# Cached keys turned on VectorE, one head at a time, instead of on TensorE: one inference step of a two-layer hybrid decoder

## The reference

```python
def moba_attend(q, kb, vb, t, slopes):
    qf = q * (B_HEAD_DIM ** -0.5)
    kbar = jnp.mean(kb.astype(jnp.float32), axis=2)
    g = jnp.einsum('hqd,hnd->hqn', qf.astype(jnp.float32), kbar)
    ...
    _, top = lax.top_k(g, min(MOBA_TOPK, NB))
    ...
    s = jnp.einsum('hqd,hqnkd->hqnk', qf, ks).astype(jnp.float32) - slopes[:, None, None, None] * dist
    s = jnp.where(valid[..., None] & (dist >= 0), s, NEG)
    p = jax.nn.softmax(s.reshape(H, q.shape[1], -1), axis=-1).reshape(s.shape)
    return jnp.einsum('hqnk,hqnkd->hqd', p.astype(vs.dtype), vs)
```

## Time and profile before

| | |
|---|---|
| median of the three runs | 1226.19 us |
| the profiled execution's own time | 1224.0 us |
| its span, first to last instruction | 1222.3 us |
| mean granted TensorE clock | 0.992 |
| TensorE busy | 1176.9 us, 96% |
| VectorE busy | 713.0 us, 58% |
| ScalarE busy | 564.2 us, 46% |
| DMA | 324.87 MB, mean 266 GB/s |
| key stage | 334.5 to 487.0 us |
| value stage | 487.0 to 634 us |

### The profile page before, as it was taken

One profiled execution on the slowest core, in us unless ns is written; L12 is line 12 of the kernel. 1 busy time (PEld: TensorE's weight loads), 2 busy tenths in 40 slices (PEclk: granted clock), 3 DMA queues, 4 the chain that ended last, 5 costly groups with the idle time before them and its releaser, 6 DMA issues.

```text
span 1222.3 us, 23737 instructions
## 1 busy us (share of the span) xinstructions
PE 1176.9 (96%) x9352; PEld 1042.2 (85%) x9352; DVE 713.0 (58%) x1355; ACT 564.2 (46%) x714; POOL 331.5 (27%) x207
## 2 busy tenths in 40 slices
PE   5899999999999999999999999899999989999997
PEld 2589798878888787787788898899999889999997
DVE  3746555545544546633545447489999996583112
ACT  3333324333354444422333237576666656575443
POOL 1000000000000002200000002667666778605773
PEclk9999999999999999999999999999999999999998
DMA  9999899999898878899999997585848445454542
GB/s 332 339 331 343 283 334 314 375 354 355 290 313 305 277 259 295 258 371 328 338 372 342 321 331 200 174 280 165 283 156 275 138 142 184 140 174 156 166 145 94
DMA packets 236962, 324.87 MB, mean 266 GB/s; under 512 B 12429, under 2 KB 152525, under 8 KB 236429
## 3 DMA queue, kind: packets, MB, share of 16 engines
q1 hardware_dynamic: 233472, 312.78, 75.7%
q0 software_dynamic: 2192, 7.79, 2.2%
q10 hardware_dynamic: 1188, 2.79, 0.7%
HBM read 317.96 MB, written 7.06 MB: 266 GB/s over the span
## 4 chain that ended last, share of the span: by engine, by line
PE 76%; DVE 16%; DMA 3%; issue 2%; ACT 2%; SPq 1%; POOL 0%; DVEq 0%; ACTq 0%
PE PS L307 19%; PE PS L311 18%; PE PS L310 18%; DVE PS L1763 10%; PE PS L395 5%; PE PS L987 4%; DMA XR<-in_ada_w 3%; PE PS L1014 3%; PE PS L1245 2%; DVE WLO L301 1%; PE PS L410 1%; SPq L382 1%; PE PS L1971 1%; ACT WHI L296 1%; DVE PS L1757 0%
## 5 line engine op out<-in xcount | busy, mean ns | idle before, releaser
L307 PE MATMUL PS<-HH,WHI 128*128 128x288 f32 x2176 | 662.4, 304 | 16.7 <-DVE HL L1683 4.5
L311 PE MATMUL PS<-HH,WLO 128*128 128x288 f32 x2176 | 643.9, 296 | 0.0
L310 PE MATMUL PS<-HL,WHI 128*128 128x288 f32 x2176 | 643.7, 296 | 0.0
L307 PEld LDWEIGHTS PS<-HH,WHI 128*128 128x128 f32 x2176 | 410.9, 189 | 38.2 <-issue 32.0
L296 ACT ACTIVATE WHI<-WRAW 128x1024 fp32r<-128x1024 f32 x272 | 283.8, 1056 | 344.1 <-PE PS L311 291.2
L310 PEld LDWEIGHTS PS<-HL,WHI 128*128 128x128 f32 x2176 | 411.2, 189 | 0.0
L311 PEld LDWEIGHTS PS<-HH,WLO 128*128 128x128 f32 x2176 | 410.6, 189 | 0.0
L301 POOL TENSOR_TENSOR WLO<-WRAW,WHI 128x1024 fp32r<-128x1024 f32 x117 | 281.1, 2422 | 192.6 <-ACT WHI L296 192.6
L301 DVE TENSOR_TENSOR WLO<-WRAW,WHI 128x1024 fp32r<-128x1024 f32 x155 | 191.1, 1235 | 158.1 <-ACT WHI L296 157.9
L1763 DVE SCALAR_TENSOR_TENSOR PS<-ACTS,CWT,PS 128x288 f32<-128x288 f32 x448 | 192.5, 516 | 0.0
L1739 ACT ACTIVATE ACTS<-ACTS 128x1088 f32<-128x1088 f32 x32 | 70.4, 2200 | 59.8 <-DVE ACTS L1761 34.6
(11 more groups left out here) (280 smaller groups left out, 748.1 us busy)
## 6 DMA issues: line engine op xcount, KB each, us to landing
XR<-in_ada_w SPq DMA_DIRECT2D x192, 512.0 KB, 8.5
WRAW<-in_ab_w_in SPq DMA_DIRECT2D x112, 512.0 KB, 7.3
WRAW<-in_c_w_in SPq DMA_DIRECT2D x96, 512.0 KB, 3.6
XR<-in_cache_b_k SPq DMA_DIRECT2D x128, 256.0 KB, 5.2
XR<-in_cache_b_v SPq DMA_DIRECT2D x128, 256.0 KB, 5.5
WRAW<-in_ab_w_out SPq DMA_DIRECT2D x32, 512.0 KB, 8.9
WRAW<-in_c_w_out SPq DMA_DIRECT2D x32, 512.0 KB, 3.3
ACTS<-in_x_prompt ACTq DMA_DIRECT2D x2, 1024.0 KB, 11.1
```

The lines of the kernel that those rows point to most:

```text
L307: first = pe.matmul(out, whi, HH[:, k, :], start=start, stop=False)
L310: pe.matmul(out, whi, HL[:, k, :], start=False, stop=False)
L311: return pe.matmul(out, wlo, HH[:, k, :], start=False, stop=stop)
```

## The change

Keys are turned by VectorE: `dve.transpose` turns 32x32 blocks, each within its group of 32 partitions, from `XR` to `KT`, two instructions of 128x512 for a head (all four samples, 256 positions each). `KT` is a ring of five slots, one head each. A key of head dimension 128 then no longer lies with its dimension down the 128 partitions: partition 32 i + d holds, for each position group i of 32, dimension 32 e + d of part e. So the query is spread block-diagonally into `BD` (`q_spread` on TensorE, `q_fill` on VectorE and ScalarE), and a head's scores are 16 matmuls of 64 columns (four samples, four parts e of the dimension). A row of the scores (sample, parity of the head, position group, token) now holds a quarter of a block, 64 positions, for each of the four head pairs side by side; four rows make one softmax. Gate, maximum and sum over the four rows are made by small TensorE operations (`gate_sum`, `max_turn`, `max_back`, `z_sum`), and the probabilities are scaled by ScalarE (`row_norm`) before they are turned. The turning is 36 steps (`probs_turn`), two at a time behind a part (`probs_pair`).

Two heads are scored behind every fourth part. Both slots of a half are released together, when its fourth head has been turned. For b = 0 the probabilities are turned in block 7 and in the first value chunk, for b = 1 in value chunks 8 to 10, and branch A's steps move behind them, its statistic to blocks 3 to 7. The page numbers are read behind the last pages of the block before, in the value stage too. `SBUF` room for the ring (3072 columns) comes from a smaller scratch area for software DMA.

```diff
         HL = sb("HL", [P, KC, R], F32R)
-        NACT = 56 * R
+        NACT = 56 * R + 3072
...
-        KT = A(6912, 4096).rearrange("p (b j h n) -> p b j h n", b=2, j=4, h=2)
...
+        BD = A(5632, 3072).rearrange("p (x w) -> p x w", w=48)
+        OQ = A(5632, 768).rearrange("p (j g w) -> p j g w", j=4, g=4)
+        KT = [A(at, 1024).rearrange("p (x n) -> p x n", x=8) for at in (8704, 9728, 56 * R, 56 * R + 1024, 56 * R + 2048)]
...
+        SROW = [A(at, 4 * 288).rearrange("p (h c) -> p h c", h=4) for at in (3456, 13824)]
...
-        def k_turn(pe, u, c, g4):
...
-            for h2 in range(2):
-                for t in range(2):
-                    at = 512 * (2 * j2 + t) + P * ((2 * hh + h2) % 4)
-                    last = pe.transpose(PS[:, (M2, M3)[g % 2], (2 * h2 + t) * P:(2 * h2 + t + 1) * P],
-                                        XR[:, c, at:at + P], IDENT[:])
-            last.then_inc(kt_tr, 1)
...
+        def k_turn(dve, u, h):
+
+            n, half = 8 * u + h, h // 4
+            if h % 4 == 0:
+                dve.wait_ge(x_rdy[2 * half], need(17 + u, 2 * half))
+                dve.wait_ge(x_rdy[2 * half + 1], need(17 + u, 2 * half + 1))
+            if n >= len(KT):
+                dve.wait_ge(ks_head, n - len(KT) + 1)
+            for c in range(2):
+                dve.transpose(KT[n % len(KT)][:, 4 * c:4 * c + 4, :],
+                              XR[:, 2 * half + c].rearrange("p (a n) -> p a n", a=4)[:, :, P * (h % 4):P * (h % 4) + P]
+                              ).then_inc(kt_tr, 1)
+            if h % 4 == 3:
+                dve.wait_ge(kt_tr, 2 * n + 2)
+                dve.sem_inc(x_used[2 * half], 1)
+                dve.sem_inc(x_used[2 * half + 1], 1)
+
+        def q_spread(pe, b, e):
+
...
+            rhs = Q[:, :, SR0 + 16 * b:SR0 + 16 * b + 16].rearrange("p h (s i) -> p s h i", i=DS)
+            for i in range(4):
+                dst = PS[32 * i:32 * i + 32, M3, P * e:P * e + P].rearrange("p (s h i) -> p s h i", s=4, h=HEADS)
+                last = pe.matmul(dst, IDENT[:, 32 * e:32 * e + 32], rhs, start=True, stop=True)
+            last.then_inc(s_qr, 1)
+
+        def q_fill(eng, b, tokens, pairs=range(4)):
+
+            eng.wait_ge(s_qr, 4 * b + 4)
+            if b:
+                eng.wait_ge(ks_head, 28 if pairs[0] == 0 else 32)
...
+                eng.wait_ge(s_bdz, 1)
+            g0, g1 = pairs[0], pairs[-1] + 1
+            for i in tokens:
+                src = PS[32 * i:32 * i + 32, M3, :].rearrange("p (x g h q) -> p x g h q", g=4, h=2, q=DS)
+                for h2 in range(2):
+                    at = 32 * h2 + DS * i
+                    dst = BD[32 * i:32 * i + 32, :, at:at + DS].rearrange("p (x g) q -> p x g q", g=4)[:, :, g0:g1]
+                    if tokens[0]:
+                        eng.activation(dst, src[:, :, g0:g1, h2, :], ACT.Copy).then_inc(s_bda, 1)
+                    else:
+                        eng.tensor_copy(dst, src[:, :, g0:g1, h2, :]).then_inc(s_bdf, 1)
...
+        def k_scores(pe, u, h):
+
+            g, h2, bank = h // 2, h % 2, (M0, M2)[u % 2]
+            n = 8 * u + h
+            pe.wait_ge(kt_tr, 2 * n + 2)
+            if h == 0:
+                if u > 1:
+                    pe.wait_ge(ks_free, u - 1)
+                if u % 4 == 0:
+                    pe.wait_ge(s_bdf, 4 + u)
+                    pe.wait_ge(s_bda, 4 + u)
+            if u == 4 and h == 4:
+                pe.wait_ge(s_bdf, 12)
+                pe.wait_ge(s_bda, 12)
+            for e in range(4):
                 for j in range(4):
-                    last = pe.matmul(PS[32 * j:32 * j + 32, M0, 0:BLOCK], QM[:, j, h, :], KT[:, hh % 2, j, h2, :],
-                                     start=h == 0, stop=h == HEADS - 1)
+                    x = (4 * e + j) * 4 + g
+                    last = pe.matmul(PS[32 * j:32 * j + 32, bank, 64 * g:64 * g + 64], BD[:, x, 16 * h2:16 * h2 + 32],
+                                     KT[n % len(KT)][:, 2 * j:2 * j + 2, 32 * e:32 * e + 32],
+                                     start=h2 == 0 and e == 0, stop=h2 == 1 and e == 3)
             last.then_inc(ks_head, 1)
...
+        def probs_turn(pe, b, t, g):
+
+            f = t // 4
...
+            for i in range(4 if t < 8 else 1):
+                dst = PS[32 * i:32 * i + 32, probs_bank(b, f), (t % 4) * P:(t % 4 + 1) * P]
+                last = pe.matmul(dst.rearrange("p (j r) -> p j r", j=4)[:, :, 8 * g:8 * g + 8],
+                                 SROW[b][:, g, 32 * t:32 * t + 32], rows[:, i], start=True, stop=True)
+            if t in (3, 7, 8) and g == 3:
+                last.then_inc(s_ptt, 1)
+
+        def probs_pair(pe, b, y):
+
+            for x in (2 * y, 2 * y + 1):
+                probs_turn(pe, b, x // 4, x % 4)
...
             for u in range(8):
-                for c in range(4):
-                    pe.wait_ge(x_rdy[c], need(17 + u, c))
...
-                    for g4 in range(4):
-                        k_turn(pe, u, c, g4)
-                        n, g = 16 + 2 * u + c // 2, 4 * (c % 2) + g4
-                        rest_part(pe, n, g, x_used[c] if g4 == 3 else None)
-                        if g == 0 and n > 16:
-                            k_scores(pe, (n - 17) // 2, 2 * ((n - 17) % 2) + 1)
-                        if g == 6:
-                            k_scores(pe, u, c - 1)
...
+                for s in range(16):
+                    rest_part(pe, 16 + 2 * u + s // 8, s % 8)
+                    if u == 0 and s < 4:
+                        q_spread(pe, 0, s)
+                    if s % 4 == 3 and u + s // 8:
+                        for h in (s // 2 - 1, s // 2):
+                            k_scores(pe, u if s > 8 else u - 1, h % 4 if s > 8 else 4 + h)
+                    if u == 3 and 10 < s < 15:
+                        q_spread(pe, 1, s - 11)
+                    if (u, s) == (4, 13):
+                        gate_sum(pe, 0)
...
         def scores_take(dve, u):
             b, tp = u // 4, u % 4
-            dve.wait_ge(ks_head, 4 * u + 4)
...
-                                     ALU.mult, ALU.add).then_inc(ks_free, 1)
+            dve.wait_ge(ks_head, 8 * u + 8)
+            src = PS[:, (M0, M2)[u % 2], 0:BLOCK].rearrange("p (h c) -> p h c", h=4)
+            dve.tensor_reduce(GATE[:, :, tp], src, AX.X, ALU.add)
+            dve.tensor_tensor(SROW[b][:, :, 64 * tp:64 * tp + 64], src, ALB, ALU.add).then_inc(ks_free, 1)
...
+                        q_fill(dve, 1, (0, 1), (0, 1))
+                    if (u, c) == (4, 2):
+                        q_fill(dve, 1, (0, 1), (2, 3))
+                    if u and c == 2:
+                        scores_take(dve, u - 1)
+                    k_turn(dve, u, 2 * c)
+                    k_turn(dve, u, 2 * c + 1)
+                    if (u, c) == (0, 0):
+                        q_fill(dve, 0, (0, 1))
                     if c % 2 == 0:
                         lo(dve, 67 + 2 * u + c // 2)
...
         def v_pe(pe):
             for m in range(32):
                 v, half = m // 4, m % 4 // 2
-                rest_chunk(pe, 32 + m)
+                for g in range(8):
+                    rest_part(pe, 32 + m, g)
+                    if m == 0 and g % 4 == 3:
+                        k_scores(pe, 7, 3 + g // 2)
+                        k_scores(pe, 7, 4 + g // 2)
+                    if m == 0:
+                        probs_pair(pe, 0, 9 + g)
+                    if m in (8, 9):
+                        probs_pair(pe, 1, 8 * (m - 8) + g)
+                if m == 0:
+                    probs_pair(pe, 0, 17)
...
+            regs = page_numbers(sp, 1)
             for s in range(32):
                 u, c = s // 4 + 1, s % 4
-                if c == 0:
-                    regs = page_numbers(sp, u % 8)
                 load_pages(sp, 16 + u, u, regs, c, kc_v if u < 8 else vc_v)
+                if c == 3:
+                    regs = page_numbers(sp, (u + 1) % 8)
                 if s % 2:
                     w_load(sp, 72 + s // 2)
...
-                if half == 0 and v < 8:
-                    regs = page_numbers(sp, v)
                 for c in (2 * half, 2 * half + 1):
                     if v < 8:
                         load_pages(sp, 24 + v, v, regs, c, vc_v)
                     else:
                         load_ada(sp, 32, 16, c)
+                if half and v < 7:
+                    regs = page_numbers(sp, v + 1)
                 w_load(sp, 89 + 2 * k)
```

432 lines of the change are left out of this document (244 added, 188 removed).

## The result

Four runs of the changed kernel gave a median of 1241.0 us, the kernel before, run beside it, 1230.8: a ratio of **1.0117, 95% interval 1.0068 to 1.0165**. The forecast was 1214, the range ended at 1236. The profiled execution took 1239.6 us (span 1237.9).

A forecast was written before the change was run, and what follows sets the result against it. TensorE, busy 96% of the span, bounds the kernel; in the new key stage VectorE or page loads do. 1224.0 - 14.1 (up to the first value chunk's end) + 4.2 (value stage) = 1214.1 us; range 1198 to 1236.

The forecast's parts named there:

- The turns: Key stage, VectorE: 128 transposes of 128x512, each 0.69 us like the nearest copy, 0.62 start to start.
- Rival C: Key stage: 4-byte transposes bind VectorE in every half, slower from 0.76 us start to start, 1232 to 1273; chance 0.12.
- TensorE's price of scores: Key stage: 64-column score matmuls at about 20 ns, 0.8 us a pair of heads, 26 us for 32 pairs.
- The floor: Small matmuls: the 25 ns floor refuted by 12 ns starts; by it b = 1 probabilities cost 2 us more, sum 1216.
- The page gap: Key stage: 9.3 us from a slot pair's release to both slots' landing, bounds 7.5 and 10.8; VectorE waits 8.
- Rival B: Key stage: page loads at 10.8 us and a transpose at 0.70 give 1227, no change; chance 0.12.
- The b = 0 probabilities lie in TensorE's idle time and cost nothing: Before the first value chunk's end: b = 0 probability turns fit into TensorE's idle time, price nothing.
- without that cover: Before the first value chunk's end: b = 0 probabilities would cost 4.5 us if TensorE had no idle time there.
- The value stage: TensorE binds it: 18 b = 1 probability pieces of 0.25 us, 4.5, replace 1.3 of turns; loss 4.2 us in all.
- The later stages do not change: Behind the value stage: no change, no term in the sum.
- The page numbers at nothing: Sync queue: page-number loads moved behind the previous block's last pages; at most 8.1 us per half, so nothing added.
- rival D: Key stage: TensorE's granted clock falls, 5 us lost at block ends, 1219; chance 0.08.

The follow-up runs named there:

- probs_grouped: The changed kernel with the 18 pieces of the b = 1 probabilities in one row behind value chunk 9; 1240.2 us, ratio 1.0119 to the kernel before.
- short_pages: The changed kernel, but pages of seven of the eight key blocks bring 8 of their 128 rows; 1229.7 us, ratio 1.0017 to the kernel before.
- probs_thin: The changed kernel with only three b = 0 probability pieces and one of four matmuls in each b = 1 piece; 1232.5 us, ratio 1.0061 to the kernel before.
- short_thin: The changed kernel with both leave-outs: 8 of 128 rows of the key pages, and thinned probability turns; 1219.6 us, ratio 0.9928 to the kernel before.
- scratch_only: The kernel before with only the scratch ring for GpSimd's software-made DMAs cut to 4096 bytes; 1233.5 us, ratio 1.0047.
- numbers_only: The kernel before with only the page-number loads moved behind the previous block's last pages; 1228.4 us, ratio 1.0008.
- filler: The changed kernel with one to four unread matmuls ahead of each pair's scores in blocks three to eight; 1246.7 us, ratio 1.014 to the kernel before.
- fours_early: The changed kernel with probability pieces of 16 matmuls and both convolution state loads on GpSimd, allowed four weight loads earlier; 1248.5 us, ratio 1.0146 to the kernel before.

## Why the prediction was wrong

From 1214.1 to the profiled 1239.6 it is 25.5 us: 1.6 of start, 16.0 in K + V0 (156.9 for the 140.9 that the forecast implied), 3.9 in V, 4.2 in O (25.7 by these rounded figures). Step by step:

- **The turns: right.** 0.678 us, 0.60 start to start. Rival C needed 0.76.
- **TensorE's price of scores: somewhat low, and near by luck.** It is 0.92 for a pair, 29 ns a matmul, for a forecast 0.8 and 20; at the lower clock 1.7 (491.57 to 493.27), for 1.3. Both rows that it was interpolated from were miscounted, since a float32 matmul stands in them as two records. The 64 of the earlier trace rows in 0.77 us are 32 matmuls, 24 ns each with the last one's tail, and the 16 of L1014 in 1.01 are 8, 126 ns each and not 63. By columns, 64 of them would then have come to about 39 ns, 1.4 us a pair.
- **The floor: rightly refuted, by a wrong figure.** The Trainium skill (TensorE: Matmul & The Clock Gate, "Wait — 56ns, not 53.3ns?") gives a floor of about 25 ns between the starts of small matmuls. The prediction held it to be refuted by 12 ns. By the right count the pairs' scores lie above it. The 32 of the earlier trace rows lie below it all the same, their first and last record starting 0.57 us apart, 18 ns a matmul, and so do the 92 of the dense row of probs_grouped, 1.63 us apart, 18 ns each.
- **The page gap: mis-sized.** 10.8 us from the first issue and 11.4 from the release, for 9.3. The step failed at the landing above all: it gave the last page of a pair the median of all pages, and in all 14 pairs the page issued last landed last, 6.6 us after its issue. In the kernel before the last of each eight pages took 6.3 on average, so this could have been read ahead. Waits were 20.8 us instead of 8. With the pages nearly gone most of the waits went, and K fell by 13.5 (short_pages). Rival B had nearly the right gap, and with 1227 was still too low for lack of the next point.
- **"The b = 0 probabilities lie in TensorE's idle time and cost nothing": wrong.** Of the terms put at nothing this is the largest, 11.1 us by probs_thin. The idle time ends when the last block's first pages are in (468.8), and the pieces stand right there: from 468.7 on the matmul timeline is without a gap up to the two stops of V0, which hold 3.2 us. TensorE, which I had dropped as a bound of this stage, was the bound of its end. The forecast gave it 9.6 us in each block, 77 in all; it was busy 113 of 143 us. Even the price "without that cover", 4.5, was too low.
- **What the rest was worth: right in the sum.** Without its 8 us of page waits the forecast has 132.9 for K + V0; short_thin, which has hardly any page waits and hardly any pieces, has 130.7.
- **The value stage: right in kind, a piece mis-sized.** 0.43, not 0.25, on 18 pieces (the last two stand together) is up to 3.2 of the 3.9 missed. I had added the matmuls to the 0.16 of the earlier trace rows; probs_thin shows that a piece costs the same with two of them as with eight.
- **"The later stages do not change": wrong.** The cut scratch ring was in the diff and I gave it no price. scratch_only shows it to cost 5.6 in the kernel before, enough for the 4.2, and TensorE waits for the second load in both.
- **The page numbers at nothing: right in the kernel before** (numbers_only); in the changed kernel they hold 1% of the chain, about 10 us of it between 336 and 500 us. Eight of them stand ahead of the second block's first pages (346.4 to 350.5), behind a weight load that waits up to 345.96: the slots were released at 348.3 and the first page issued at 350.9. Their move was not undone there, so what it costs stays open.
- **The clock, rival D: not decided.** The clock fell in the key stage as D said. In V0 it cost an estimated 2.4 us: three parts with their pieces at 1.39 instead of 0.85, one pair's scores at 1.70 instead of 0.92. The filler changed too little to price the rest.

The summed misses of K + V0, 12.8 of page waits and 11.1 of pieces, are more than the 16.0 that were missed. Two things would account for it, neither shown by itself: they overlap where TensorE catches up while VectorE waits, and the remaining terms were a little too dear.

## What to carry to other kernels

Work costs nothing only where the cover stands at its own place in the order: check it at the last block, where what waits for the inputs and what fills the waits meet. Several transfers in a row are there when the last of them is, so take the landing of the last and not the median of all, and count from the release. Small matmuls of another shape between products are priced by the number of groups first, and a long row of them can stop for longer than its matmuls take (3.8 us here). A float32 matmul can stand in the records twice: count instructions in the program before dividing. An edit made only to win room, here a smaller scratch ring, needs a term of its own in the sum.

## What the runs showed that was not expected

- A piece of small matmuls between two parts costs TensorE 0.43 us, with 2 or with 8 matmuls in it; pieces of 16 come to 0.57 (1.39 us from one to the next, less two parts of 0.41).
- Rows and pieces of small matmuls stop with nothing to wait for in the program: 1.0 and 2.2 us in V0, 3.8 us after 184 records, and at one and the same instruction 0.7 and 1.8 us in two kernels. All five stops end 1.3 to 1.6 us behind the end of a 16 KB instruction load. That points to code loading as the cause, but other such loads stand beside no stop, and no run took the loads away by themselves.
- With the scratch ring at 4096 bytes the second 960 KB load of GpSimd starts 10.0 to 12.5 us after the first (14.2 in fours_early), just behind its landing, where it was 1.25 us.
- Issues of 64-row pages start 0.65 us apart (median), of 128-row pages 0.515, of 8-row pages 0.46.
- VectorE's transposes of 128x512 f32 elements take 0.678 us, as much as a copy of that size from PSUM (0.688 in the earlier trace rows).
